# Compression in the two column halves ahead of the rotations; first level's masks on GpSimd in four buffers

## The reference

```python
def compress_blocks(kv, pos_emb, w1, w2):          # once for keys, once for values
    ch = kv.reshape(B, G, S // CMP_STRIDE, CMP_STRIDE, D)
    blk = jnp.concatenate([ch[:, :, :-1], ch[:, :, 1:]], axis=3) + pos_emb
    flat = blk.reshape(B, G, -1, CMP_BLOCK * D)    # 2 groups x 31 blocks, 32*64 = 2048 wide
    return jax.nn.silu(flat @ w1) @ w2             # w1 is 2048 x 256, w2 is 256 x 64
...
    s_cmp = jnp.einsum('bgrsd,bgcd->bgrsc', qh, k_cmp) * SCALE
    p_cmp = masked_softmax(s_cmp, cmp_end[None, :] <= pos[:, None])
    q_rot = partial_rope(qh, pos)                  # keys are rotated in the same way
...
def rwkv7_step(state, inp):
    sa = jnp.einsum('bhvk,bhk->bhv', state, -kk_t)
    state = (state * w_t[:, :, None, :] + sa[..., None] * (kk_t * a_t)[:, :, None, :]
             + v_t[..., None] * k_t[:, :, None, :])
    y = jnp.einsum('bhvk,bhk->bhv', state, r_t)
```

## Time and profile before

| | |
|---|---|
| median of 3 runs | 1861.49 us (1858.94 to 1863.05) |
| profiled execution, its own time | 1861.29 us |
| its span | 1859.5 us |
| mean granted TensorE clock | 0.978 of full |
| TensorE busy | 1774.6 us, 95% |
| VectorE, ScalarE, GpSimd busy | 51%, 29%, 38% |

### The profile page before, as it was taken

One profiled execution on the slowest core, in us unless ns is written; L12 is line 12 of the kernel. 1 busy time (PEld: TensorE's weight loads), 2 busy tenths in 40 slices (PEclk: granted clock), 3 DMA queues, 4 the chain that ended last, 5 costly groups with the idle time before them and its releaser, 6 DMA issues.

```text
span 1859.5 us, 28324 instructions
## 1 busy us (share of the span) xinstructions
PE 1774.6 (95%) x11768; PEld 1426.3 (77%) x11768; DVE 956.5 (51%) x1642; ACT 535.3 (29%) x1082; POOL 701.0 (38%) x333
## 2 busy tenths in 40 slices
PE   8999998999889989889999999999998999999999
PEld 5678777877766767767888888877786688888887
DVE  6676247666646355665656561133334366565411
ACT  3111113444323445543322220034223332222100
POOL 4343101000244132135655554452224475555542
PEclk9999999999899999999999999998999899999999
DMA  5222130000132321122332323221112123232332
GB/s 172 79 80 88 32 103 3 3 2 2 59 115 73 112 85 63 40 91 70 102 102 91 103 92 101 93 94 46 62 53 68 57 93 102 93 100 94 99 100 70
DMA packets 43505, 143.54 MB, mean 77 GB/s; under 512 B 5305, under 2 KB 7115, under 8 KB 43250
## 3 DMA queue, kind: packets, MB, share of 16 engines
q1 hardware_dynamic: 43378, 141.73, 23.3%
HBM read 139.07 MB, written 4.08 MB: 77 GB/s over the span
## 4 chain that ended last, share of the span: by engine, by line
PE 63%; DVE 5%; ACT 3%; issue 1%; POOL 1%; DVEq 0%; ACTq 0%; POOLq 0%
PE all_p_bank L206 19%; PE all_p_bank L207 18%; PE all_p_bank L208 18%; DVE l_sc L2478 1%; PE all_p_bank L2177 1%; PE all_p_bank L2390 1%; PE all_p_bank L2153 1%; DVE l_mx L2484 1%; PE all_p_bank L2419 0%; PE all_p_bank L2857 0%; PE all_p_bank L1904 0%; PE all_p_bank L2852 0%; DVE b_whi L180 0%; PE all_p_bank L2839 0%; POOL b_wlo L187 0%
## 5 line engine op out<-in xcount | busy, mean ns | idle before, releaser
L187 POOL TENSOR_TENSOR b_wlo<-b_raw,b_whi 128x1024 fp32r<-128x1024 f32 x238 | 580.6, 2443 | 782.7 <-DVE b_whi L180 778.8
L206 PE MATMUL all_p_bank<-b_hi,b_whi 128*128 128x512 f32 x1248 | 507.6, 407 | 11.4 <-issue 6.1
L207 PE MATMUL all_p_bank<-b_lo,b_whi 128*128 128x512 f32 x1248 | 489.6, 392 | 0.0
L208 PE MATMUL all_p_bank<-b_hi,b_wlo 128*128 128x512 f32 x1248 | 489.5, 392 | 0.0
L180 DVE CAST b_whi<-b_raw 128x1024 fp32r<-128x1024 f32 x238 | 186.2, 789 | 447.8 <-PE all_p_bank L208 430.3
L206 PEld LDWEIGHTS all_p_bank<-b_hi,b_whi 128*128 128x128 f32 x1248 | 236.5, 189 | 80.1 <-issue 25.4
L208 PEld LDWEIGHTS all_p_bank<-b_hi,b_wlo 128*128 128x128 f32 x1248 | 236.2, 189 | 51.0
L207 PEld LDWEIGHTS all_p_bank<-b_lo,b_whi 128*128 128x128 f32 x1248 | 236.5, 189 | 50.3 <-issue 5.1
L206 PE MATMUL all_p_bank<-f_mhi,b_whi 128*128 128x512 f32 x352 | 136.9, 389 | 0.0
L207 PE MATMUL all_p_bank<-f_mlo,b_whi 128*128 128x512 f32 x352 | 136.9, 389 | 0.0
L208 PE MATMUL all_p_bank<-f_mhi,b_wlo 128*128 128x512 f32 x352 | 136.9, 389 | 0.0
(11 more groups left out here) (452 smaller groups left out, 2667.1 us busy)
## 6 DMA issues: line engine op xcount, KB each, us to landing
b_raw<-in_w_up SPq DMA_DIRECT2D x88, 512.0 KB, 3.6
b_raw<-in_w_down SPq DMA_DIRECT2D x44, 512.0 KB, 3.7
b_raw<-in_w_in SPq DMA_DIRECT2D x32, 512.0 KB, 3.7
b_raw<-in_w_out SPq DMA_DIRECT2D x24, 512.0 KB, 3.7
b_raw<-in_w_gla SPq DMA_DIRECT2D x22, 512.0 KB, 3.6
b_raw<-in_w_diff SPq DMA_DIRECT2D x20, 512.0 KB, 3.7
b_raw<-in_w_mem SPq DMA_DIRECT2D x8, 512.0 KB, 3.8
all_x<-in_x SPq DMA_DIRECT2D x8, 256.0 KB, 5.4
```

What stands on the lines that cost most here:

```text
L187: self.nc.gpsimd.tensor_tensor(self.lo[:, n % SLOTS, :], self.raw[:, n % RAWS, :], self.hi[:, n % SLOTS, :].bitcast(F32), ALU.subtract).th ...
L206: nc.tensor.matmul(acc, lhsT=left[0], rhs=right[0], start=first, stop=False)
L207: nc.tensor.matmul(acc, lhsT=left[0], rhs=right[1], start=False, stop=False)
L208: return nc.tensor.matmul(acc, lhsT=left[1], rhs=right[0], start=False, stop=last)
```

## The change

`Sparse.order` begins with the inputs, and keys and values go through the `hidden` steps together:

```diff
-    order = [("rope", 0, 0), ("rope", 1, 0), ("gates", 0, 0), ("inputs", 0, 0), ("inputs", 1, 0)]
-    order += [("hidden", 0, i) for i in range(4)] + [("plain", 0, 0), ("hidden", 1, 0), ("hidden", 1, 1), ("lift", 0, 0)]
-    order += [("hidden", 1, 2), ("hidden", 1, 3), ("plain", 1, 0), ("keys", 0, 0), ("lift", 1, 0)]
+    order = [("inputs", 0, 0), ("inputs", 1, 0), ("hidden", 0, 0), ("rope", 0, 0), ("hidden", 0, 1), ("rope", 1, 0)]
+    order += [("hidden", 0, 2), ("gates", 0, 0), ("hidden", 0, 3), ("plain", 0, 0), ("lift", 0, 0), ("keys", 0, 0)]
...
-    def hidden(self, pe, kv, i):
+    def hidden(self, pe, i):
         m = self.m
         if i == 0:
-            pe.wait_ge(self.s_xp, 4 * kv + 4)
-        pe.wait_ge(self.i_w1[i], 16 * kv + 16)
+            pe.wait_ge(*self.projected)
+            pe.wait_ge(self.s_xp, 8)
+            pe.wait_ge(self.s_pad, 1)
+        pe.wait_ge(self.i_w1[i], 32)
         for j in range(4 * i, 4 * i + 4):
-            mm = self.nc.tensor.matmul(self.b[kv][0:2 * CMP_N, 0:CMP_H], lhsT=m.xp[:, kv, :, :, j].rearrange("p g c -> p (g c)"),
-                                       rhs=m.w1[:, j, :], start=(j == 0), stop=(j == CMP_B // 2 - 1))
+            for kv, rows in enumerate(HALVES):
+                mm = self.nc.tensor.matmul(self.b[0][rows, 0:CMP_H], lhsT=m.xp[:, kv, :, j], rhs=self.weights_of(kv, i)[:, j % 4, :],
+                                           start=(j == 0), stop=(j == CMP_B // 2 - 1))
         mm.then_inc(self.s_h, 1)
```

`xp` is padded from 62 to 64 columns (GpSimd sets the padding to zero), so one `plain`, one `lift` (two transposes of 128x128) and one Silu serve both. `inputs` 0 now writes the four blocks that need no data from the other half of the partitions (keys and values), `inputs` 1 the four that do:

```diff
-    def inputs(self, dve, kv):
+    def inputs(self, dve, cross):
+
         m = self.m
-        if kv == 0:
+        if cross == 0:
+            dve.wait_ge(*self.projected)
             dve.wait_ge(self.i_pos, 16)
-            dve.wait_ge(self.s_rot, 2)
-        for cross in range(2):
+        for kv in range(2):
```

Three pieces of the values' weights have places of their own, so seven pieces are issued at once and the eighth after the first `hidden` step:

```diff
-        for i in range(4):
-            self.load(sp, 0, i)
+        for kv, i in ((0, 0), (1, 0), (0, 1), (1, 1), (0, 2), (1, 2), (0, 3)):
+            self.load(sp, kv, i)
...
     def sync(self, sp):
         for what, n, i in self.order:
-            if what == "hidden" and n == 0:
-                sp.wait_ge(self.s_h, i + 1)
-                self.load(sp, 1, i)
+            if what == "hidden" and i == 0:
+                sp.wait_ge(self.s_h, 1)
+                self.load(sp, 1, 3)
```

In the recurrence all 24 masks move to GpSimd. Those of level 0 are put in its order at `pair` 8, 10, 12 and 14, and go to four buffers (`mb[0]`, `mb[1]`, `g[0]`, `g[1]`). `level_g` of level 0 transposes `w` (mask + identity), and ScalarE writes the result straight to `z`, so L1643 is gone. The addition `s1` of each chunk moves to GpSimd as well:

```diff
     def gpsimd(self, pool):
         m = self.m
         for what, n, i in self.order:
+            if what == "pair" and n == 8:
+                pool.wait_ge(self.i_sm, 16)
+                pool.wait_ge(self.i_la, 16)
+                pool.wait_ge(*self.projected)
+            if what == "pair" and n in (8, 10, 12, 14):
+                pool.wait_ge(self.s_pc, n - 6)
+                self.masked(pool, n // 2 - 4)
+            if what == "level" and n + 4 < 4 * self.levels and n < 2:
+                self.masked(pool, n + 4)
+            if what == "level" and 6 <= n + 1 < 4 * self.levels:
+                self.masked(pool, n + 1)
+            if what == "as" and n < NCH - 1:
+                pool.wait_ge(self.s_st, n + 1)
+                if n:
+                    pool.wait_ge(self.s_tmp, n)
+                self.nc.gpsimd.tensor_tensor(m.s1[:, :, :], m.s[:, n % 2, :, :], m.kv[:, :, n, :], ALU.add
+                                             ).then_inc(self.s_s1, 1)
...
     def level_g(self, pe, n):
         m, lv, i = self.m, n // 4, n % 4
-        pe.wait_ge(self.s_mb, n + 1)
+        if lv:
+            pe.wait_ge(self.s_mb, n + 1)
+        else:
+            pe.wait_ge(self.s_wv, n + 1)
...
             if what == "level":
                 if n == 0:
                     dve.wait_ge(self.s_pc, 16)
-                    self.masked(dve, 0)
                 if n >= 6:
                     self.update(dve, n - 2)
-                if n + 1 < 4 * self.levels:
-                    self.masked(dve, n + 1)
                 if n < 4:
                     self.update(dve, n)
...
         if lv == 0:
             dve.wait_ge(self.s_mb, n + 1)
-            nc.vector.tensor_tensor(m.w[:, i, :, :], m.mb[:, n % 2, :, :], eye, ALU.add).then_inc(self.s_wv, 1)
-            dve.wait_ge(self.s_gc, n + 1)
-            nc.vector.tensor_tensor(m.z[:, i, :, :], m.g[:, n % 2, :, :], eye, ALU.add).then_inc(self.s_z, 1)
+            nc.vector.tensor_tensor(m.w[:, i, :, :], self.near(n), eye, ALU.add).then_inc(self.s_wv, 1)
             return
```

More of the change, by code:

```diff
@@ L724, in __init__ @@
         self.sc, self.pt = s.sb("sc", [P, 32, 32]), s.sb("pt", [P, 8, P])
+        self.w1v = [at("v", where, f"w1v{i}", [P, 4, CMP_H]) for i, where in enumerate((a + 20480, a + 24576, a + 4096))]
         self.apt = at("n", s.at, "apt", [P, 2, T])
@@ L810, in gpsimd @@
         for what, n, i in self.order:
+            if what == "inputs" and n == 0:
+                pool.wait_ge(*self.projected)
+                nc.gpsimd.memset(m.xp[:, :, 2 * CMP_N:HD, :], 0.0).then_inc(self.s_pad, 1)
             if what == "rope":
@@ L847, in tensor @@
             if what == "hidden":
[L848 removed]
+                self.hidden(pe, i)
             if what == "lift":
[L850 to L851 removed]
+                pe.wait_ge(self.s_plain, 1)
                 for ht in range(2):
[L853 to L854 removed]
+                    mm = nc.tensor.transpose(b[0][:, CMP_H + ht * P:CMP_H + ht * P + P], m.plain[:, ht * P:ht * P + P],
+                                             k["ident"][:, :])
                 mm.then_inc(self.s_ht, 1)
@@ L1068, in inputs @@
                 self.nc.vector.tensor_tensor(
-                    m.xp[rows, kv, g, :, :], ap, m.pos[rows, kv, :].unsqueeze(1).broadcast_to([64, CMP_N, CMP_B // 2]),
-                    ALU.add).then_inc(self.s_xp, 1)
+                    m.xp[rows, kv, CMP_N * g:CMP_N * g + CMP_N, :], ap,
+                    m.pos[rows, kv, :].unsqueeze(1).broadcast_to([64, CMP_N, CMP_B // 2]), ALU.add).then_inc(self.s_xp, 1)
     def masked(self, dve, half):
@@ L1337, in level_g @@
             pe.wait_ge(self.s_gc, n - 1)
-        if lv:
-            pe.wait_ge(self.s_z, n - 3)
+        if lv >= 2:
+            pe.wait_ge(self.s_z, n - 7)
         for c in range(NCH):
             for rows in HALVES:
+                left = m.mb[rows, n % 2, c, :] if lv else m.w[rows, i, c, :]
                 rhs = m.z[rows, i, c, :] if lv else self.k["ident"][rows, rows]
-                mm = self.nc.tensor.matmul(self.b[n % 2][rows, CH * c:CH * c + CH], lhsT=m.mb[rows, n % 2, c, :], rhs=rhs,
-                                           start=True, stop=True)
+                mm = self.nc.tensor.matmul(self.b[n % 2][rows, CH * c:CH * c + CH], lhsT=left, rhs=rhs, start=True, stop=True)
         mm.then_inc(self.s_lg, 1)
@@ L1350, in level_d @@
         if lv < self.levels - 1:
-            pe.wait_ge(self.s_z, n)
+            if n == 4:
+                pe.wait_ge(self.s_pc, 16)
+            else:
+                pe.wait_ge(self.s_z, n - 4)
             for c in range(NCH):
@@ L1626, in mask, with near, masked @@
         return v.unsqueeze(1).broadcast_to([P, NCH, CH])
-    def masked(self, dve, n):
+    def near(self, n):
+        return (self.m.g if n in (2, 3) else self.m.mb)[:, n % 2, :, :]
+    def masked(self, pool, n):
         m, lv, i = self.m, n // 4, n % 4
-        if n >= 2:
-            dve.wait_ge(self.s_lg, n - 1)
-        if 2 <= n < 6:
-            dve.wait_ge(self.s_wv, n - 1)
-        self.nc.vector.tensor_tensor(m.mb[:, n % 2, :, :], m.abk[:, 0, i, :, :], self.mask(lv), ALU.mult).then_inc(self.s_mb, 1)
+        if n >= 6:
+            pool.wait_ge(self.s_lg, n - 1)
+        elif n >= 4:
+            pool.wait_ge(self.s_wv, n - 3)
+        self.nc.gpsimd.tensor_tensor(self.near(n), m.abk[:, 0, i, :, :], self.mask(lv), ALU.mult).then_inc(self.s_mb, 1)
     def update(self, dve, n):
```

40 lines of the change are left out of this document (25 added, 15 removed).

## The result

The changed kernel takes 1865.1 us (median of 11 runs, 1862.5 to 1869.1) against 1858.3 for the kernel before in as many runs beside it: a ratio of 1.0036, 95% interval 1.0024 to 1.0049, so 6.8 us or 0.36% slower. The forecast was 1860.9, no change; 1865.1 lies at the slow end of its range for 8 in 10. In the profiled execution the difference is 1867.34 - 1861.29 = 6.05 us.

What follows compares the result with a forecast made beforehand. TensorE, busy 95% of the span, was taken as the bound, except VectorE from 266.1 to 299.3 us. First merge +0.7, masks -0.3, `s1` -0.8: -0.4 on 1861.29 gave 1860.9 us; 8-in-10 range 1855.5 to 1866.

Steps and rivals of the forecast that it cites:

- The start: Compression's start: TensorE idles 9.6 us waiting for inputs, first `hidden` step at 239.9 against 237.28, steps 1.73 + 0.17 us each.
- Its clock: Behind the idle start: first `hidden` step at half speed for 3.0 us, costing 1.5 us, bounds 0 to 3.4.
- Scores to first level: From scores near 266 to the first `level_g` at 285 to 286, with 2.35 us lost to GpSimd.
- The two masks beside the softmax: GpSimd's third and fourth mask stretch VectorE's softmax operations: 0.5 us on L1095, 1.2 on the two small ones.
- The first `w`: Before the first level: VectorE's first `w` loses 0.65 us behind GpSimd's addition of rotation 3.
- First level to merge: Level 0 to first merge: 13.6 us at full clock, plus 1.7 for one 3.4-us spell at 0.50; merge at 300.85.
- Behind the merge: Levels and chunks after the first merge: 0.3 us gained by moved masks and 0.8 by `s1`.
- -0.7: At the first merge: a slow spell in the kernel before still slowed that merge by 0.7 us, setting its comparison at 300.14.
- -0.3: Levels and chunks: the other 18 masks leave VectorE, gaining 0.3 us, with 0 and 1.8 as ends.
- The 0.8 of `s1`: Levels and chunks: `s1` on GpSimd lets `rhs` start earlier where TensorE waits, gaining 0.8 us, 0 to 1.
- the slower one: Rival: slow clock lasts, two more spells in compression or levels, 3.4 us, plus 1.2 of collisions: 1865.5 us; chance 0.15.

Runs made afterwards that it cites:

- warm_start: The changed kernel with ten matrix products that nobody reads on TensorE ahead of the first `hidden` step; 1863.3 us, 1.0009 of the kernel before.
- masks_four: The changed kernel with GpSimd's masks 0 to 3 queued at pairs 8 to 11, ahead of rotation 2's addition; 1864.0 us, 1.0011 of the kernel before.
- warm_both: The changed kernel with ten idle TensorE products ahead of the first `hidden` step and three ahead of pair 15; 1862.1 us, 1.0006 of the kernel before.
- spread_warm: spread_in with three idle TensorE products added ahead of pair 15; 1859.4 us, 0.9988 of the kernel before.
- comp_spread: The kernel before with only the compression changed, masks and `s1` still on VectorE, and the start of spread_in; 1861.2 us, 1.0008 of the kernel before.
- spread_in: The changed kernel with old start order, `pos` sent early, `inputs` in four steps between pairs, GpSimd's four masks behind pair 7's; 1860.6 us, 1.0007 of before.
- pos_rope: The changed kernel with `pos` sent early and the old order at its start, all four `hidden` steps in a row; 1864.2 us, 1.0017 of the kernel before.

## Why the prediction was wrong

- **The start: right.** With the projection 1.06 us later in this profile (its last readout ends at 230.19, before 229.13), the first `hidden` step is at 241.03 - 1.06 = 239.97; forecast 239.9. The idle time is 9.67 us; forecast 9.6. A step alone takes 2.02 us at full clock; forecast 1.73 + 0.17, start to start.
- **Its clock: mis-sized, 2.1 us for 1.5.** "I expect the first `hidden` step at half speed for 3.0 us: 1.5 us." There is a spell of 10.2. It began at 235.2, in the idle time, so 4.4 us of it fell on work. From the first `hidden` step to the scores it is 26.9 us; the sum said 24.6 + 1.5, and `warm_start` without slow clock shows 24.8. So the clock cost 2.1 us for 1.5, and the stretch came out 0.8 short.
- **Scores to first level: near.** 19.9 us against 19.5. The two masks beside the softmax cost what was said: 0.56 on L1109 (0.5 said), 1.07 on the two small ones (1.2 said, 1.34 us for 0.27 from the start of the first to the end of the second); `masks_four` got back 1.7 of the stretch. The first `w` lost 0.28 for 0.65, and VectorE waited 0.28 for pair 15, which ran at half clock; the forecast didn't have that.
- **First level to merge: this is the step that failed.** "One spell of 3.4 us at 0.50 costs 1.7 in a chain that now is TensorE's." The chain itself was right: 13.6 us was the forecast's part without clock, and `warm_both` and `spread_warm` show 13.8. The term was mis-sized: a spell of 13.7 us made it 17.1, that is 3.3 us of clock, not 1.7 (2.3 in the other profile of the same kernel). With the 0.8 of the start and 0.3 of the stretch between, the merge is 2.9 us later than forecast, and the later projection, which the change didn't touch, adds 1.06. With the 1.0 and the 1.4 of the next point that is 6.4 us, from 1860.9 to the profiled 1867.3. The forecast was made for the kernel before as profiled, 1861.29, so its difference has to be held against the 6.05 us of the profiles.
- **Behind the merge.** The forecast had -0.7 (a spell of before that would not come again), -0.3 and -0.8 there. Up to the end of the head's long wait the profile shows -0.8 in place of -1.8. The 0.8 of `s1` doesn't show: from the first `as` to the start of the last `out` product it is 80.8 and 81.0 us in two profiles of the changed kernel (clock 0.96 and 0.98) and 81.4 in two of before (0.94); at the same 0.94 it is 81.3 in `masks_four`, with `s1` on GpSimd, and 81.4 in `comp_spread`, with it on VectorE. And a step was missed: with five sparse steps fewer, one of them behind `keys`, the mixed order puts one more unit between first merge and first `pre` (160 records of L962 for 152 of L951), so 101.1 us for 99.4 (101.1 to 101.3 in every kernel with the new compression, 98.7 to 99.4 in the three with the old); it comes back behind, 27.2 us for 28.7 from the first `pre` to the first `as`. The last 1.4 of the 6.05 us lie beyond the head's long wait, where the same code took 1336.7 to 1341.7 us in the fourteen profiles: nothing shows that they belong to the change.
- **The rivals.** The outcome is nearest to the slower one, "the slow clock is not one spell but lasts", with a chance of 0.15. That 1865.1 came for its 1865.5 is in part luck: the clock cost 2.2 us more than forecast where that rival has 3.4, its 1.2 of further collisions didn't come, and in the profiled run the projection and the end of the kernel add 2.5 us that it doesn't have. What was weighed wrongly is the length of a spell. I priced each by the 3.4 us of the earlier trace rows, but the trace of the kernel before has longer ones, at 417.0, 492.1 and 1253.3 us; the first comes after 4.9 busy us in 6.5:

```profile
410.50:413.50 3.00, 3.00 (x56) 2.27 (x52) 2.13 (x7) 0.84 (x3) 0.00 (x0) 1.00 0.02 5
413.50:417.00 3.50, 1.89 (x14) 1.42 (x12) 3.43 (x11) 2.05 (x6) 0.00 (x0) 1.00 0.00 0
417.00:427.30 10.30, 8.94 (x33) 6.05 (x33) 5.36 (x15) 5.21 (x12) 0.00 (x0) 0.50 0.01 2
```

The new start has 2 busy us in 11.6, and I gave it a single short spell. Each of the six profiles in which TensorE waits 6.9 us or more for the inputs with nothing to fill it has a 10.2-us spell there; the eight others have none, 3.4 or 6.8. But the longest wait alone doesn't say how long a spell lasts: `spread_in` has 6.8 us beside waits of 1.4 us at most, and the waits around the start of the 10.2 us at 417.0 are 1.5 us at most.

The Trainium skill ("TensorE: Matmul & The Clock Gate", Part 1) says that how many matrix products at the start of a kernel run at the slow clock differs between runs of one kernel. For the share of a whole run the runs here show the like, with mean clocks of 0.973 to 0.982 for one and the same kernel. The Trainium skill ("SBUF — State Buffer", section "Who interferes with whom") says that a VectorE instruction with two inputs in SBUF contends with a GpSimd instruction that reads SBUF, and that one with a single such input, outside the two-port modes, does not. The trace agrees: L1109, L1114 and L1082 grew (1.13 to 1.69, 0.18 to 0.71 on the mean, and 0.67 to 1.63 for the longest of four in `pos_rope`), L1538 with its input in PSUM stayed at 0.69.

What stays open: how much of the difference between the two medians (6.8 and 2.1 us) belongs to draws of slow spells behind 305 us, and why those differ between kernels whose code there is the same (0.93 to 0.98). Open is also what sets the length of a spell.

## What to carry to other kernels

When a change takes work off one engine and makes TensorE wait at one place for longer, the wait can be paid twice: once as idle time (9.7 us here), once as slow clock on what follows (2.1 us here). Take the length of a slow spell from the longest ones in the trace, not from the nearest one. Before trusting "that wait is hidden", look whether TensorE has anything to do in it; here, cutting the producer's block into four with other work between, with its data sent earlier and GpSimd's masks out of the way, gave 6 to 8 us back at the merge. And masks that are moved to GpSimd "early" run when their queue lets them, not when the code says early: check what stands before them there, and which two-input operations of VectorE they then meet.

## What the hardware showed that was not expected

- Spells of 10.2 and 13.7 us at clock 0.50, the first around an idle wait of 9.7 us, the second behind a stretch of 10.9 busy us in 15.1; the forecast had priced 3.4. The first began in idle time and ran 4.4 us on into full work.
- The same 264 records of TensorE between first level and first merge took 11.0 busy us at clock 1.00 and 14.4 at 0.73.
- Matrix products of 128 rows and 64 columns with 256 moving columns, in two column halves, run side by side, two for the time of one: 16 records in 2.02 us, where 8 of 62 columns took 1.99 before, with 0.01 to 0.04 us between the starts of a pair.
- For one kernel, the mean clock goes with the time of a run: 1.87 us for each 0.001 over 105 runs.
